# Expert gates of a two-layer block: a table added up by 256 indirect transfers in place of one-hot products

## What is computed

```
s1, s2 = q1 @ sub_k1.T, q2 @ sub_k2.T        # 8 heads, 128 scores each
v1, i1 = top_k(s1, 16);  v2, i2 = top_k(s2, 16)
vs, ci = top_k(v1[:, None] + v2[None, :], 16) # 256 sums
e1, e2 = i1[ci // 16], i2[ci % 16]
eidx   = e1 * 128 + e2                        # one of 16384 experts
gates  = softmax(vs)                          # 16 per head
act    = gelu(expert_u[eidx] . x)             # 8 * 16 = 128 experts per token
out    = sum over the 128 of  act * gates * expert_v[eidx]
```

## Time and profile before

| | |
|---|---|
| time, median of 3 runs | 3005.99 us (3005.98 to 3009.66) |
| time of the profiled execution | 3007.15 us |
| its span, first to last instruction | 3005.4 us |
| TensorE busy | 2962.8 us, 99% of the span |
| VectorE busy | 2020.9 us, 67% |
| ScalarE busy | 1488.6 us, 50% |
| GpSimd busy | 169.0 us, 6% |
| the 448 instructions of L2203 (224 products, two instructions each) | 27.4 + 27.4 us of TensorE's busy time |
| granted TensorE clock | 0.998 |

### The profile page before, as it was taken

How to read it: one execution, slowest core, us unless ns; L and a number is a source line. 1 busy time by engine, 2 the same in 40 slices (tenths; PEclk the granted TensorE clock), 3 DMA queues, 4 the chain that set the end, 5 groups by cost and what they waited for, 6 DMA issues and landing times.

```text
span 3005.4 us, 42961 instructions
## 1 busy us (share of the span) xinstructions
PE 2962.8 (99%) x17085; PEld 2678.9 (89%) x17085; DVE 2020.9 (67%) x2869; ACT 1488.6 (50%) x2274; POOL 169.0 (6%) x312
## 2 busy tenths in 40 slices
PE   8999999999999999999999999999999999999999
PEld 7998778888888888978789999999999999999999
DVE  5656654444445445554557988888888888888876
ACT  4355544444444444454444466447745555555553
POOL 2000000000000002140000000000010000000000
PEclk9999999999999999999999999999999999999999
DMA  7554355556554554535667779778999899899764
GB/s 255 160 169 154 114 169 193 189 188 193 184 195 182 194 189 150 169 109 208 190 208 249 237 261 338 238 222 293 337 371 360 300 328 321 310 322 318 264 221 141
DMA packets 238382, 690.73 MB, mean 230 GB/s; under 512 B 14249, under 2 KB 95177, under 8 KB 203392
## 3 DMA queue, kind: packets, MB, share of 16 engines
q1 hardware_dynamic: 221024, 598.71, 59.2%
q0 software_dynamic: 12608, 71.73, 6.3%
q10 hardware_dynamic: 4576, 17.89, 1.6%
HBM read 652.61 MB, written 33.57 MB: 228 GB/s over the span
## 4 chain that ended last, share of the span: by engine, by line
PE 51%; DVE 0%; ACTq 0%; ACT 0%; issue 0%; DVEq 0%
PE banks L2156 16%; PE banks L2232 14%; PE banks L2157 8%; PE banks L2233 7%; PE banks L2203 2%; PE banks L2253 1%; PE banks L2255 1%; PE banks L2254 1%; PE banks L2175 0%; DVE peer_features L378 0%; DVE weights_lo L195 0%; PE banks L2192 0%; PE banks L2221 0%; ACTq L2310 0%; DVE residual L2585 0%; DVE peer_scratch L2584 0%
## 5 line engine op out<-in xcount | busy, mean ns | idle before, releaser
L195 DVE TENSOR_TENSOR weights_lo<-weights,weights_hi 128x1024 fp32r<-128x1024 f32 (+4 forms) x1080 | 1228.5, 1179 | 701.8 <-ACT weights_hi L188 700.0
L188 ACT ACTIVATE weights_hi<-weights 128x1024 fp32r<-128x1024 f32 (+4 forms) x1080 | 1046.4, 1017 | 1316.8 <-PE banks L419 640.8
L2156 PE MATMUL banks<-peer_features,weights_hi 128*128 128x448 f32 (+1 forms) x2304 | 738.9, 377 | 2.7 <-DVE weights_lo L195 2.7
L417 PE MATMUL banks<-weights_hi,features_hi 128*128 128x512 f32 (+3 forms) x1600 | 605.2, 378 | 12.5 <-DVE weights_lo L195 9.3
L2157 PE MATMUL banks<-peer_features,weights_lo 128*128 128x224 f32 (+1 forms) x2304 | 615.3, 267 | 0.0
L419 PE MATMUL banks<-weights_hi,features_lo 128*128 128x512 f32 (+3 forms) x1600 | 600.5, 375 | 0.0
L418 PE MATMUL banks<-weights_lo,features_hi 128*128 128x512 f32 (+3 forms) x1600 | 600.4, 375 | 0.0
L2232 PE MATMUL banks<-peer_features,weights_hi 128*128 128x448 f32 x1568 | 492.4, 374 | 0.0
L2156 PEld LDWEIGHTS banks<-peer_features,weights_hi 128*128 128x128 f32 x2304 | 432.0, 187 | 44.2 <-DVE weights_lo L195 3.2
L2157 PEld LDWEIGHTS banks<-peer_features,weights_lo 128*128 128x128 f32 x2304 | 438.6, 190 | 0.0
L2233 PE MATMUL banks<-peer_features,weights_lo 128*128 128x224 f32 x1568 | 414.3, 264 | 0.0
(11 more groups left out here) (406 smaller groups left out, 2757.7 us busy)
## 6 DMA issues: line engine op xcount, KB each, us to landing
weights<-in_expert_u SPq DMA_DIRECT2D x128, 1024.0 KB, 5.5
weights<-in_expert_v SPq DMA_DIRECT2D x128, 1024.0 KB, 7.2
weights<-in_w_ffn_gate SPq DMA_DIRECT2D x44, 1024.0 KB, 5.1
weights<-in_w_ffn_up SPq DMA_DIRECT2D x44, 1024.0 KB, 5.1
weights<-in_w_ffn_down SPq DMA_DIRECT2D x44, 1024.0 KB, 4.8
weights<-in_w_in SPq DMA_DIRECT2D x48, 900.0 KB, 4.7
weights<-in_w_out SPq DMA_DIRECT2D x32, 1024.0 KB, 5.1
weights<-in_w_in SPq DMA_DIRECT2D x24, 704.0 KB, 4.2
```

The costliest lines, as they stand in the source:

```text
L188: act.activation(hi[:, k, n], raw[:, k, n], ACT.Copy).then_inc(self.hi_ready, 1 + skip)
L195: last = dve.tensor_tensor(lo[:, k, n], raw[:, k, n], hi[:, k, n].bitcast(F32), ALU.subtract)
L417: pe.matmul(out, xh, wh, start=first, stop=False)
L2156: pe.matmul(self.bank(n % 3, 2 * (T - lo)), wh[:, k, :], F[:, k, :, lo:T], start=(k == 0), stop=False)
```

## The change

The gates are no longer made by products. A table in DRAM, 16 MB with one cell for each pair of keys and token (all 256 tokens), is set to zero: GpSimd clears one buffer of 8 KB per partition, and SyncE writes it out 16 times at 1 MB, one at each f from 2 to 17, behind that f's weights. While choosing, VectorE works out for each slot the number of its cell, (e2 * 128 + e1) * 256 + token, with two small operations for each part. GpSimd then issues, for each of the 256 slots of the two halves, one indirect transfer that adds 128 single gates, one per token, into the table. Two heads can choose the same expert, so GpSimd waits before each head's 16 transfers until all earlier ones have landed; within a head no cell is named twice.

The order on GpSimd is: three gathers, then scatters 1 to 224, then for each further gather four of the last 32 scatters until they are through. Gather number 3 (the fourth) stands behind 224 scatters.

The steps move: the second half is chosen from step 56 (before: 74), and the product sums, which had steps 56 to 73 and 108 to 141, now have 90 to 141. So row 3 is first needed in step 96. The final loads fetch the table in pieces of 8 KB per partition (1 MB each).

```diff
-        SC, RET, TURN = 18, (22, 74), (55, 107)
+        SC, RET = 18, (22, 56)
-        HOT = [(58 + i, 0, ROWS // 8 + i) for i in range(16 - ROWS // 8)] + [(110 + i, 1, i) for i in range(16)]
-        SUM = [56, 57, *range(58, 74), *range(108, 142), *range(V0 - 1, V0 + 8), *range(V0 + 9, V0 + 12)]
+        SUM = [*range(90, 142), *range(V0 - 1, V0 + 8), *range(V0 + 9, V0 + 12)]
...
+        g_rows = nc.dram_tensor("expert_gates", (P * NKEYS * T, 1), F32, kind="Internal").ap()
+        g_d = g_rows.rearrange("(p e t) o -> p e (t o)", e=NKEYS, t=T)
+        ZEROED = 8
...
+                    ch(dve.tensor_scalar(vif[:, 0:2, :].rearrange("p h k -> p (h k)"), eg[:, 0, slots], float(T), token[:, t:t + 1],
+                                         ALU.mult, ALU.add))
+                    ch(dve.scalar_tensor_tensor(out=cell_of[:, t, slots], in0=eg[:, 1, slots], scalar=float(NKEYS * T),
+                                                in1=vif[:, 0:2, :].rearrange("p h k -> p (h k)"), op0=ALU.mult, op1=ALU.add))
...
+                        if 0 <= f - 2 < NKEYS // ZEROED:
+                            sp.wait_ge(zeros_made, 1)
+                            sp.dma_start(g_d[:, ZEROED * (f - 2):ZEROED * (f - 1), :],
+                                         rows[:, 2, :].rearrange("p (e t) -> p e t", t=T)).then_inc(zeroed, 16)
...
-                            sp.dma_start(g_in[g % 2], g_d[:, :, 8 * g:8 * g + 8, :]).then_inc(g_back[g % 2], 16)
+                                sp.wait_ge(scattered, 16 * NT * SLOTS)
+                            sp.dma_start(g_in[g % 2], g_d[:, 8 * g:8 * g + 8, :]).then_inc(g_back[g % 2], 16)
...
+                    def scatter(t, slot):
+                        if slot % TOPK == 0:
+                            pool.wait_ge(chosen, PARTS * t + slot // (HP * TOPK) + 1)
+                            if t + slot > 0:
+                                pool.wait_ge(scattered, 16 * (SLOTS * t + slot))
+                        pool.indirect_dma_start(out=g_rows[:, :], in_=gates_of[:, t, slot:slot + 1], in_offset=None, compute_op=ALU.add,
+                                                out_offset=bass.IndirectOffsetOnAxis(ap=cell_of[:, t, slot:slot + 1], axis=0))\
+                            .then_inc(scattered, 16)
+
+                    pool.wait_ge(zeroed, 16 * NKEYS // ZEROED)
+                    for c in range(BUFS):
+                        gather(c)
+                    scatters = [(t, slot) for t in range(NT) for slot in range(SLOTS)]
+                    late = HP * TOPK
+                    for t, slot in scatters[:-late]:
+                        scatter(t, slot)
+                    for c in range(BUFS, 2 * ROWS):
+                        gather(c)
+                        for t, slot in scatters[len(scatters) - late + 4 * (c - BUFS):][:4] if c - BUFS < late // 4 else ():
+                            scatter(t, slot)
...
-                        if n in TURN:
-                            if n > BACK[-1]:
-                                pe.wait_ge(*x_back(KD // 2))
-                            pe.wait_ge(chosen, TURN.index(n) + 1)
-                            for c in range(3):
-                                last = pe.transpose(self.bank(5, P, c * P), eg[:, c, :], self.ident[:, :])
-                            last.then_inc(choice_turned, 1)
...
-                        for t, r, place_in_order in hot_step(n):
-                            for g in (2 * r, 2 * r + 1):
...
-                                for c in range(4):
-                                    last = pe.matmul(self.bank(3 + g % 2, P, c * P), h[:, 0, c, :], h[:, 1, c, :],
-                                                     start=True, stop=True)
-                                last.then_inc(gated, 1)
...
```

More of the change, by code:

```diff
@@ L1927, in peer @@
             skT = scratch[:, 4096:6144].rearrange("p (j n) -> p j n", j=PQ_TILES)
-            gblk = scratch[:, 0:4096].rearrange("p (b e t) -> p b e t", b=2, t=BLK)
-            hot = [x.rearrange("p (g w c e) -> p g w c e", g=2, w=2, c=4) for x in (XN[:, 0, :], scratch[:, 4096:6144])]
             s_in = [XN[:, 1 - b, 0:8 * DENSE].rearrange("p (e t) -> p e t", t=DENSE) for b in range(2)]
-            g_in = [scratch[:, b * 2048:b * 2048 + 8 * DENSE].rearrange("p (b e t) -> p b e t", b=BLKS, t=BLK) for b in range(2)]
+            g_in = [scratch[:, b * 2048:(b + 1) * 2048].rearrange("p (e t) -> p e t", t=T) for b in range(2)]
             S = tmp("peer_scores", [P, 2, 2, DENSE])
@@ L2024, in tail @@
                     ch(dve.tensor_tensor(g, g, sm[:, :].unsqueeze(2).to_broadcast([P, HP, TOPK]), ALU.mult))
+                    dve.sem_inc(chosen, 1)
                 for part in range(PARTS):
@@ L2098, in _ @@
                         if f == SCORES_AT:
-                            sp.wait_ge(chosen, NT)
+                            sp.wait_ge(chosen, NT * PARTS)
                             for b in range(2):
@@ L2127, in _, with gather @@
                     pool.sem_inc(counted, 1)
+                    pool.memset(rows[:, 2, :], 0.0).then_inc(zeros_made, 1)
+                    self.pool_chain.on(pool)(pool.iota(token_i[:, :], pattern=[[P, NT]], base=0, channel_multiplier=1))
+                    self.pool_chain.on(pool)(pool.tensor_copy(token[:, :], token_i[:, :]))
+                    pool.sem_inc(counted, 1)
                     self.rstd_of_tiles(pool, D)
-                    for c in range(2 * ROWS):
+                    def gather(c):
                         if c % 8 == 0 and c < ROWS:
@@ L2193, in _ @@
                             last.then_inc(self.turned.sem, 1)
[L2194 to L2207 removed]
+                    pe.wait_ge(spread_read, 1)
                     pe.wait_ge(*x_back(KD // 2))
@@ L2438, in leave @@
                                           ALU.add).then_inc(tile_read, 1)
-                    def one_hots(g, gi):
-                        if gi >= 4:
-                            dve.wait_ge(gated, gi - 3)
-                        h = hot[g % 4 // 2][:, g % 2]
-                        dve.tensor_tensor(h[:, 0], iof[:, :].unsqueeze(1).to_broadcast([P, 4, P]),
-                                          egT[:, 1, 4 * g:4 * g + 4].unsqueeze(2).to_broadcast([P, 4, P]), ALU.is_equal)
-                        for c in range(4):
-                            if c in by_act:
-                                continue
-                            tok = slice(4 * g + c, 4 * g + c + 1)
-                            last = dve.tensor_scalar(h[:, 1, c, :], iof[:, :], egT[:, 0, tok], egT[:, 2, tok],
-                                                     ALU.is_equal, ALU.mult)
-                        last.then_inc(hots, 1)
                     def feature_lo(j):
@@ L2539, in _ @@
                             ch(dve.tensor_tensor(row_gate[:, 0, :], row_gate[:, 0, :], row_gate[:, 1, :], ALU.mult))
-                        for t, r, place_in_order in hot_step(s):
-                            if place_in_order == 0 or (t == 1 and r == 0):
-                                dve.wait_ge(choice_read, t + 1)
-                            for g in (2 * r, 2 * r + 1):
-                                one_hots(g, 2 * place_in_order + g % 2)
                         if s > V0 and (s - V0) % 8 == 0:
```

75 lines of the change are left out of this document (14 added, 61 removed).

## The result

The changed kernel took 3166.15 us, the median of 4 runs (3162.29 to 3172.96); the kernel before took 3006.41 beside it (3005.98 to 3009.66, 4 runs). The ratio is 1.053, 95% interval 1.0516 to 1.0541. I had forecast 2979 us and a range up to 3075. The kernel is 160 us slower, and on the side that rival B described, at a price above B's highest.

The account below looks back on a forecast made before the run. TensorE, busy 99% of the span, bounds the kernel: 50.8 us taken off it, less one 24.0 us stall for the late fourth gather, gives 26.8 us less than 3005.99, 2979 us; range 2955 to 3075.

Parts of the forecast that it names:

- rival B: Wait in step 96: adding makes scatters dear, p 1.44 to 1.59, 47 to 81 us slower; 35% with long-tail rival.
- What bounds the kernel: Expert stage: TensorE, busy 99% of the span and without gaps from 1616 us; work added elsewhere is free until it waits.
- 50.8 us off TensorE: Gate products on TensorE: 28 pieces of 1.79 us, 50.1, and two turnings of the choice, 0.7, go.
- DMA and moved steps at nothing: Writes of zeros, larger final loads and moved choosing and sums: all put at 0 us, hidden behind TensorE.
- The deadline: Fourth gather, step 96: VectorE's sum possible at 1968.6 us, 3.0 us of slack, so needed by 1971.6 us.
- The arrival's start: GpSimd, first half's gates and cells: ready for the first scatter at 1671.6 us.
- L: GpSimd's wait from the end of issuing a head's last scatter until it lands, 13 times: 5 us, bounds 3.3 and 7.5.
- p: GpSimd: time from one scatter to the next, taken from the gathers as 1.11 us, 224 times ahead of the fourth gather.
- Bounds: Limits on the time between scatters on GpSimd: 1.08 us below, 1.44 above, from the gathers' rows.
- L by the rule: GpSimd's landing wait by the skill's fixed cost: about 2 us, so no stall and the full 50.8 us gained.
- Break-even: Wait in step 96: with L = 5 the 50.8 us gain is used up at p = 1.23.

Follow-up runs that it names:

- experiment 1: Against the changed kernel, none of the 256 scatters is issued, the rest of the change stays: 2958.02 us, ratio 0.984 to the kernel before.
- experiment 2: Against the changed kernel, the same 256 indirect transfers write their cells in place of adding: 3083.32 us, one run.
- experiment 6: Against the changed kernel, only 128 scatters stand ahead of gather 3, the others in sixes behind gathers 3 to 24: 3095.72 us, one run.
- the mixture: Against the kernel before, first half's gates through 128 scatters into an 8 MB table, second half keeps one-hot products: 2986.92 us, ratio 0.993.

## Why the prediction was wrong, step by step

- **What bounds the kernel, and 50.8 us off TensorE.** Right: experiment 1 gave 51.2 in the span.
- **DMA and moved steps at nothing.** Right for the time (no new gap before 1967 us, and none in any window of experiment 1 from 1616 us on). The zeros held the first gather until 1651.1 us (1630.7 before), still 20 us ahead of the first scatter. The final loads took 13.4 us to land, 13.7 before, and stayed hidden.
- **The deadline.** Right: sum of step 96 possible from 1967.8 us (1968.6 forecast); TensorE's one long wait was 198.3 against VectorE's 201.3, so the slack was the 3.0 us that I worked out.
- **The arrival's start, and L.** First scatter 1671.46 us (1671.6). L was 3.1 in the mean for 5, and the gather landed 5.5 us after its issue rather than 10.4: together 30 us in the kernel's favour.
- **p: the step that failed.** "I take p = 1.11. Bounds: 1.08 below, 1.44 above." It was 2.02, and 224 x 0.91 = 204 us. With the measured values the same sum gives 224 x 2.02 + 39.8 + 1671.6 + 5.5 - 1971.6 = 198 us late, as seen. Three things are in the 0.91. First, 0.44 for the addition and what else parts it from the gathers' mean: 1.55 against 1.11 (0.58 against a plain write, experiment 2). Second, the 0.30 us of gap, which I saw ahead of the second and third gather and argued away by two *direct* transfers; it stands behind every indirect one. Third, about 0.17 from work on VectorE (shown in experiment 6) and isolated gaps (unexplained).
- **Bounds.** The upper bound of 1.44 was a gather's spacing; it held no price for the addition at all, though rival B had argued one. The range, cut at 3075, left out B's own upper end.
- **Rival B.** Right in place and kind. Its price for an index worked out twice, 1.59 us, is near the 1.55 measured, but I let it stand for the whole spacing; with the gap it would have been 1.89, and by my own sum with L = 5 some 199 us late and 148 slower, 3154 us. That the addition is a second index worked out is not shown: only that it costs 0.58 us with 128 rows and that a part of it is paid per instruction. The Trainium skill (Collectives: The Full Stack, "The bandwidth ceiling") speaks of two source reads for a transfer that adds; the issue grew from 0.97 to 1.55 us, so the runs agree in direction and not with a doubling. What the DMA engines read for an addition no run here shows.
- **L by the rule.** The Trainium skill (DMA: Bandwidth & Descriptors, "Anatomy of one DMA — SWDGE path") would have put L at about 2 us. With all else at rest 2.1 to 2.3 was measured, so there the trace agrees; beside the kernel's weights it was 2.4 to 5.7.
- **Break-even.** With the L and landing measured, the gain is used up at 224p + 39.8 + 5.5 - 300 = 50.8, so p = 1.36. The addition is above it even bare, at 1.55 + 0.30 = 1.85. A plain write is at it: 0.97 + 0.30 = 1.27 bare, 1.10 + 0.30 = 1.40 by the mean issue of experiment 2, and there it brought the stop of weights besides. What stays open: the isolated gaps, which of VectorE's instructions slow a scatter and how, and the stop of weights in experiment 2.

## What to carry to other kernels

Before work is handed to an idle engine, count its instructions and price their spacing, gap included, from the nearest rows of the *same* kind; an operation that the trace does not show (here an addition) needs a bound that contains its price, not the price of its neighbour. A queue in order turns a harmless length into a stop as soon as one instruction with a deadline stands behind it: work out how many fit ahead of the deadline (here some 120 of 256) and move just so many. That gave the mixture its 0.7%, where all of it cost 5.3%. And add up what the bottleneck engine loses, not what the engine in front of it waits: in experiment 6 VectorE waited 162.7 us, TensorE stood 94.2 and lost 45.3 more at the lower clock.

## What the hardware showed unexpectedly

- An indirect transfer issued from GpSimd: 0.97 us of issue for a write of 128 single elements, 1.55 us with an addition, 1.40 with 64 elements; 0.30 us of gap behind each one. With 128 cells it is the issue that bounds it, at some 15 ns an element (1.85 us over 128), gap included.
- The issue is slower beside a busy VectorE: 1.56 us in the mean without work of VectorE beside it, at a DMA share of 0.93, and 1.94 beside splits and product sums at 0.54 (experiment 6); 1.73 to 1.75 in the mean beside choosing and splitting (the changed kernel).
- Plain 4-byte writes into DRAM went with waits of ScalarE for weights of up to 18.6 us, 140.8 us in all (experiment 2, one run); with adding ones, slower to issue, there was none of these.
- The stop took TensorE's granted clock from 1.00 to 0.51 (1.2 GHz for 2.4); it was back at 0.96 in the mean of the 78 us behind it. The 19 stops of experiment 6 had it at 0.79 to 0.94 in windows of 80 us, and TensorE was busy for 45.3 us longer with the same instructions.
